# Half swaps of rotated keys and queries: from SyncE's DMA queue to GpSimd's, and a later load of shared keys

## The reference, cut to what matters

```python
def rope(x, pos):
    ...
    x1, x2 = xf[..., :half], xf[..., half:]
    return jnp.concatenate([x1 * cos - x2 * sin, x2 * cos + x1 * sin], axis=-1).astype(x.dtype)

def second_block(x, meta_tokens, ...):
    h = jnp.concatenate([filler, meta, x], axis=1)
    for l in range(DEPTH):
        u = rms_norm(h, pre_mix_gain[l])
        proj = u @ w_in[l]
        qa, ka, va, qb, kb, vb, g = jnp.split(proj, SPLITS, axis=-1)
        qa = rope(qa.reshape(B, Lp, SWA_Q_HEADS, HEAD_DIM), pos)
        ka = rope(ka.reshape(B, Lp, SWA_KV_HEADS, HEAD_DIM), pos)
        qb = rope(qb.reshape(B, Lp, DIFF_HEADS, 2, HEAD_DIM), pos)
        kb = rope(kb.reshape(B, Lp, DIFF_HEADS, 2, HEAD_DIM), pos)
        o_swa = windowed_gqa_sink_attention(qa, ka, va, attn_sink[l], pos, is_real)
        o_diff = differential_attention(qb, kb, vb, lam, lambda_init, subln_gain, is_key)
        ...
```

## Time and profile before

| | us |
|---|---|
| median of 3 runs | 872.35 (872.23 to 873.35) |
| the profiled execution | 872.91 |
| its span, first to last instruction | 871.1 |

### The profile page before, as it was taken

The page is one execution under the profiler, slowest core; times in us unless marked ns, Lnnn a source line. Parts: engine busy times, 40 slices in busy tenths (PEclk is TensorE's granted clock), DMA queues, the critical chain, the costliest instruction groups (busy, mean ns, idle before and its releaser), DMA issues.

```text
span 871.1 us, 13102 instructions
## 1 busy us (share of the span) xinstructions
PE 860.1 (99%) x4820; PEld 737.0 (85%) x4820; DVE 626.5 (72%) x985; ACT 468.2 (54%) x756; POOL 68.8 (8%) x96
## 2 busy tenths in 40 slices
PE   8999999999999999999998999999999999999997
PEld 6887788888888888889998888888888888888886
DVE  5867677766876666668687887887766876666665
ACT  6646534434644444445565887676653654444443
POOL 0000010000200000002142010132300100000000
PEclk9999999999999999999999999999999999999999
DMA  8965344554565555352788435755474365455431
GB/s 326 390 238 186 122 169 146 193 187 151 185 242 193 193 193 193 144 193 67 246 279 308 147 107 177 255 177 197 150 285 172 121 225 188 175 198 188 184 142 48
DMA packets 31774, 167.21 MB, mean 192 GB/s; under 512 B 4128, under 2 KB 5920, under 8 KB 14320
## 3 DMA queue, kind: packets, MB, share of 16 engines
q1 hardware_dynamic: 29280, 160.22, 51.7%
q10 hardware_dynamic: 2448, 6.37, 2.3%
HBM read 157.02 MB, written 3.83 MB: 185 GB/s over the span
## 4 chain that ended last, share of the span: by engine, by line
PE 96%; DMA 2%; DVE 1%; ACT 0%; SPq 0%; issue 0%; DVEq 0%; ACTq 0%
PE ps L526 18%; PE ps L528 18%; PE ps L527 18%; PE ps L692 8%; PE ps L677 8%; PE ps L696 4%; PE ps L673 4%; PE ps L705 3%; PE ps L1764 2%; PE ps L707 1%; PE ps L561 1%; PE ps L1698 1%; DMA kswap<-kraw 1%; PE ps L1722 1%; PE ps L1717 1%; PE ps L1712 1%
## 5 line engine op out<-in xcount | busy, mean ns | idle before, releaser
L1866 DVE TENSOR_TENSOR wlo<-raw,whi 128x2048 fp32r<-128x2048 f32 x134 | 306.8, 2291 | 148.5 <-ACT whi L871 148.0
L871 ACT ACTIVATE whi<-raw 128x2048 fp32r<-128x2048 f32 x134 | 256.4, 1914 | 183.0 <-PE ps L528 105.8
L526 PE MATMUL ps<-whi,xT 128*128 128x512 f32 x192 | 76.8, 400 | 0.0
L528 PE MATMUL ps<-whi,xT 128*128 128x512 f32 x192 | 75.0, 391 | 0.0
L527 PE MATMUL ps<-wlo,xT 128*128 128x512 f32 x192 | 74.8, 390 | 0.0
L526 PE MATMUL ps<-whi,fT_h 128*128 128x512 f32 x128 | 50.2, 392 | 0.0
L528 PE MATMUL ps<-whi,fT_l 128*128 128x512 f32 x128 | 49.8, 389 | 0.0
L527 PE MATMUL ps<-wlo,fT_h 128*128 128x512 f32 x128 | 49.8, 389 | 0.0
L1333 POOL TENSOR_TENSOR stat<-stat,cst 128x1 f32<-128x1 f32 x10 | 9.9, 1003 | 490.0 <-DVE stat L1886 260.9
L526 PE MATMUL ps<-x_all,whi 128*128 128x272 f32 x160 | 46.4, 290 | 0.0
L527 PE MATMUL ps<-x_all,whi 128*128 128x272 f32 x160 | 46.1, 288 | 0.0
(11 more groups left out here) (349 smaller groups left out, 1879.0 us busy)
## 6 DMA issues: line engine op xcount, KB each, us to landing
raw<-weights SPq DMA_DIRECT2D x134, 1024.0 KB, 4.8
kB<-key_parts SPq DMA_DIRECT2D x20, 272.0 KB, 3.3
kswap<-kraw SPq DMA_DIRECT2D x26, 136.0 KB, 2.6
key_parts<-knat SPq DMA_DIRECT2D x4, 544.0 KB, 5.5
cst<-consts SPq DMA_DIRECT2D x1, 1371.0 KB, 13.2
raw<-weights SPq DMA_DIRECT2D x4, 256.0 KB, 5.8
raw<-weights SPq DMA_DIRECT2D x2, 512.0 KB, 7.7
gate_a<-gain_rows ACTq DMA_DIRECT2D x2, 512.0 KB, 7.5
```

Source lines behind the costliest of these rows:

```text
L526: pe.matmul(o, lh, rh, start=first, stop=False)
L528: return pe.matmul(o, ll, rh, start=False, stop=last)
L871: act.activation(whi[s][:], raw[s][:], ACT.Copy).then_inc(split_hi, 1)
L1866: dve.tensor_tensor(wlo[s][:], raw[s][:], whi[s][:], ALU.subtract).then_inc(split_lo, 1)
```

## The change

The swaps move from SP to GpSimd, into one list with the low parts: for each m2 GpSimd first does the low part of blob m2-2 and then issues the swap of blob m2. The waits of a swap are the same as before. SP's list keeps its order without the swaps. The second half of the shared keys is loaded at m = 16 in place of m = 13.

```diff
-            def swap_halves(m2):
-                sp.wait_ge(taken_d if m2 in QUERIES else taken_a, taken_by(16 + m2))
-                b = m2 % 2
-                if swaps_before(m2):
-                    sp.wait_ge(kt_ok, max(turned_place(m) for m in SWAPPED if m < m2 and m % 2 == b))
-                sp.dma_start(kswap[b][0:DH], kraw[b][DH:P]).then_inc(ks_in[b], 16)
-                sp.dma_start(kswap[b][DH:P], kraw[b][0:DH]).then_inc(ks_in[b], 16)
...
-                if m - 4 in SWAPPED:
-                    swap_halves(m - 4)
                 if m - 6 in KEY_BLOBS:
                     store_keys(KEY_BLOBS.index(m - 6))
-                if m in (11, 13):
-                    load_shared_keys((m - 11) // 2)
+                if m in (11, 16):
+                    load_shared_keys((m - 11) // 5)
...
-            for m2 in SWAPPED:
+            def swap_halves(m2):
+                pool.wait_ge(taken_d if m2 in QUERIES else taken_a, taken_by(16 + m2))
+                b = m2 % 2
+                if swaps_before(m2):
+                    pool.wait_ge(kt_ok, max(turned_place(m) for m in SWAPPED if m < m2 and m % 2 == b))
+                pool.dma_start(kswap[b][0:DH], kraw[b][DH:P]).then_inc(ks_in[b], 16)
+                pool.dma_start(kswap[b][DH:P], kraw[b][0:DH]).then_inc(ks_in[b], 16)
+
+            def low_part(m2):
                 pool.wait_ge(rot_hi, turned_place(m2))
...
+            for m2 in range(20):
+                if m2 - 2 in SWAPPED:
+                    low_part(m2 - 2)
+                if m2 in SWAPPED:
+                    swap_halves(m2)
```

## The result

| | before | after |
|---|---|---|
| median of the runs, us | 872.85 (872.23 to 874.13) | 878.55 (877.97 to 880.17) |
| profiled execution, us | 872.91 | 877.97 |
| its span, us; mean granted clock | 871.1; 0.999 | 876.1; 0.997 |

The ratio after to before is 1.0073, with an interval of 1.0061 to 1.0084: 5.7 us slower on the medians (four runs of each), 6.4 by the ratio, 5.1 in the profiled executions. The forecast was 870.25 with a range that ended at 874.0.

What follows compares the result with a forecast made beforehand. TensorE's 2.23 us of waits, from blob 9's late swap, was taken as the bound; less 0.13 for thin margins, a 2.1 us gain took 872.35 to 870.25 us, all else counted as nothing; range 869.8 to 874.0.

Steps and rivals of the forecast that it cites:

- What bounds the kernel: Between 400 and 560 us TensorE loses 2.23 us in two waits, 0.80 and 1.43, both rooted in blob 9's late swap.
- GpSimd's issues: GpSimd issues two swap DMAs in each of 13 places, taken at 1.3 us each, with bounds of 0.49 and 2.65.
- the sum: Blob 9's swap lands at 463.6 us, DVE starts 2.34 us sooner, both TensorE waits go: 2.1 us gained after 0.13 off.
- the rival of slow issuing: GpSimd's issues take up to 3.6 us, held by DVE's splits; 875.4 us at 3.5; chance 0.17, of which 0.13 above 874.1.
- The landing: Blob 9's swap takes 2.6 us from issue to landing, the median of the 26 DMAs; 6.2 would leave no gain.
- A queue of its own removes the line ahead of it, not the traffic: On GpSimd's queue blob 9's swap could pass the queued load: landing 463.6 us with whole gain, or else 467.2 with none.
- At least 1.09 us earlier: SP, rid of the swaps, issues blob 13's load at least 1.09 us before its 456.52 us; off the path.
- The first swap: Blob 0's swap, behind GpSimd's norms and memsets, lands at 415.5 us; DVE stands 1.7 us; taken as nothing for TensorE.
- Blob 2's swap: DVE's wait for it, 0.85 us at 422.31, may become some 3 us; taken as covered.
- covered: Early delays at blobs 0 and 2 cost TensorE nothing, as low parts are made one and a half blobs ahead of use.
- The shared keys: Their second half, loaded behind blob 16's load, still comes 34 us ahead of need: nothing on the path.
- Same engines, same lateness: Blob 9's swap lands late, at 467.2 us, since the DMA engines are full: 872.35 to 872.95 us; chance 0.16.

Runs made afterwards that it cites:

- e8_first: The kernel before with the swap of blob 9 issued ahead of the load of blob 13 on SP: 870.70 us, ratio 0.9977.
- e11_both: The kernel before with blob 9's swap ahead of blob 13's load and the shared keys' second half behind blob 16's load, all on SP: 871.06 us, ratio 0.9981.
- e7_order: The kernel after, with SP waiting for GpSimd's signal that a swap is issued before it stores keys or issues the next load: 873.11 us, ratio 1.0008.
- e2_act: The kernel after with the swaps issued on ScalarE's hardware queue in place of GpSimd's: 878.81 us, ratio 1.0073.
- e4_before16: The kernel before with only the second half of the shared keys moved, to behind blob 16's load: 872.26 us, ratio 1.0001.

## Why the prediction was wrong, step by step

*What bounds the kernel: right.* Blob 9's late swap held 2.23 us of TensorE. e8_first and e11_both make that swap land in 3.0 us and gain 2.0 and 1.7 us by their ratios (0.9977 and 0.9981); e11_both moves the shared keys too, which alone give nothing.

*GpSimd's issues: the size was off, in the harmless direction.* 0.53 and 0.52 us, close to the lower bound of 0.49 and not 1.3. The step lacked one thing: where its own low part is the last thing it waits for, GpSimd stands 0.56 us on its own semaphore before the swap. Together 0.56 + 0.53 + 0.52 = 1.6 us, less than the 2.6 taken. With the landing of 2.6 the sum would have come out the better for it. (A landing counts from the start of its issue, 458.92 + 7.65 = 466.57 in the earlier trace rows; the sum added it behind the end of the second issue, and so took one issue too many, to the same side.) No issue was lengthened beside DVE's splits: blob 4's two, at 430.36 and 430.89, took 0.53 and 0.52 us beside the split of 430.32 to 432.61. So the rival of slow issuing fell with its mechanism.

*The landing: this step failed.* The sum put 2.6 us from issue to landing, since half of the swaps of before made it in that. But they did so in the order that SP's wait gave them. The step that moved the swaps said of SP that nobody waits for its queue directly and that its loads come earlier, and called it off the path, even a help. It then kept the landings of a trace in which those loads came later. In after blob 4's swap took 7.8 us, blob 7's 7.9; e7_order, which only restores the order of issue, brings them to 2.6 and 3.4 and the time to 1.0008.

The 2.6 was also the wrong row for the swap that the gain hung on. It is the median of all 26 DMAs; from blob 8's on the three pairs in the crowd took 5.1, 6.2 and 5.3 us, and with a queue of its own and the old order (e7_order) blob 9's took 6.4. So the two parts of the miss are these: no gain was to be had from the queue (1.0008), and the loads let forward lost the rest (to 1.0073).

*"A queue of its own removes the line ahead of it, not the traffic": half right.* The traffic stayed and so did the line. In e7_order blob 9's swap landed in 6.4 us behind a load in the other queue, 6.2 behind it in the same.

The two rules of the Trainium skill, DMA: Bandwidth & Descriptors, that were set against each other there, "Queues, rings and completion order" (turns between queues at packet granularity) and "Issuing engines are not separate DMA queues" (only issue time is saved), both have a share in what the traces show. Turns are seen in e2_act, but of whole transfers as it looks, so that a small transfer behind a load of 1 MB saved nothing in e7_order (6.4 against 6.2 us); the outcome is that of the second rule.

*"At least 1.09 us earlier": right where the stage was still on time, wrong for the load that it named, and the wrong thing to be glad of.* The second load at 430 us went out by 432.96 where it stood behind 436.29 before: over 3 us. But blob 13's load was issued at 461.42, 4.9 us later than the 456.52 of before: by then the chain of late swaps held SP too, through the stores of keys and queries ahead of that load.

*The first swap: late by nothing.* It was forecast at 415.5; issued at 409.90 and landed in 2.4 us, it was there before DVE came at 413.45, since the issues are short. Blob 2's swap made DVE wait 2.74 us where some 3 were forecast, and TensorE had no stall near 421, as forecast. But "covered" was judged by TensorE alone. That wait put blob 4's swap 1.5 us later (430.36 against 428.85), in a roundabout way. ScalarE's high part and the start of GpSimd's low part stayed where they were (426.84 and 426.79). DVE's split behind its turn moved from 424.71 to 426.28, and beside it GpSimd's pass took 3.01 us in place of 1.36. Before:

```profile
424.71 2.28 DVE L1866 TENSOR_TENSOR wlo<-raw,whi 128x2048 fp32r<-128x2048 f32 x1
426.84 1.36 POOL L1366 TENSOR_TENSOR knat<-kswap,knat 128x544 fp32r<-128x544 f32 x1 [7.53 <-ACT knat L1112]
```

and after, beside GpSimd's row at 426.79 above:

```profile
426.28 2.28 DVE L1871 TENSOR_TENSOR wlo<-raw,whi 128x2048 fp32r<-128x2048 f32 x1
```

The low part ended 1.6 us later, and the 0.56 came on top. What was covered for TensorE was not covered for the next swap of the same parity. That the store is ahead of that swap comes of the same end: both wait for the low part that ends at 429.80, SP issues at 429.82, and GpSimd stands the 0.56 us first.

*The shared keys: nothing, as said* (e4_before16, 1.0001).

*The rivals.* "Same engines, same lateness" had the mechanism, and its price was the failure: it let one swap be 0.6 us later and ended at 872.95. It moved the swap and left all else where it was. Priced with the loads moved forward, the pairs of the chain lose 5 us of landing each (2.7 to 7.8, 2.4 to 7.4, 2.9 to 7.9; one 2.8, 3.9 to 6.7), and the distance of one and a half blobs by which these parts run ahead, which covers one such loss, doesn't cover a sum of them: the first stall of TensorE stands at 458 us, 28 us after the first late swap. The side on which this could end slower than 874.1 had a chance of 0.13, all of it given to slow issuing, which didn't happen.

*The clock: not thought of.* After 2.84 us of idle TensorE came a granted clock of 0.65 over 4 us, some 1.5 us that no wait shows.

## What to carry to other kernels

A wait that a queue of bulk loads makes for a small transfer isn't only a cost to SP: it keeps the loads behind the transfer that others wait for. Before taking it away, list what that queue will issue in the meantime, in bytes, and put it ahead of the small transfer, whatever queue that one goes to; where one small transfer is late, move it ahead of the load in the order of issue (one pair of issues exchanged, -0.2% here) rather than to another engine. And a price read from the trace of before, as a median landing, holds only while the order of issue that it was measured in does.

## What the runs showed of the hardware that was not expected

Two queues didn't share the 16 engines evenly. In after, blob 4's swap was issued at 430.36 and 430.89 on GpSimd's queue, and that queue moved nothing before 435.5; SP's moved the store and a load. The queues from 435 to 437 us, and from 437 to 439:

```profile
q1 hardware_dynamic: 69, 0.44, 65.3%
q0 software_dynamic: 86, 0.26, 41.2%
...
q0 software_dynamic: 9, 0.02, 3.0%
```

Nearly all of its 0.27 MB then moved in 2 us. On ScalarE's queue (e2_act) the first half moved 2 us after its issue, as soon as the store was through, and the second after a load. That a turn is one transfer's share of an engine fits both; it is read from two places only and no run tests it; what makes GpSimd's queue miss the first turn is open (it was issued 0.5 us after the store, ScalarE's 0.06).

A small copy of half the partitions, 136 KB, costs GpSimd 0.52 to 0.54 us to issue (the first of the kernel 0.73), no more than SP (0.46 to 0.61). A swap that waits for GpSimd's own low part is issued 0.56 us after it, ten times in after.
